# A two-block, one-core kernel: the second block's first norm scaled behind its matrix units, and a layer norm about a half mean

## What is computed

```
x1 = rmsnorm(x0, final_norm_g)                       # end of the first block
h  = rmsnorm(x1, l0_norm_mix)                        # start of the second
p  = h @ l0_w_in                                     # 14 x 128 columns of rwkv, then q, k, v of 512 each
p_rwkv = p_rwkv + (shift(p_rwkv) - p_rwkv) * mu      # shift: by one token
...
u  = glu(h4 @ pw1 + pw1_b)                           # second layer, 1024 channels
u  = causal depthwise conv of 31 taps over u, + dw_b
mean, var over the 1024 channels
u  = silu((u - mean) * rsqrt(var + 1e-5) * ln_w + ln_b)
x  = x + u @ pw2 + pw2_b
```

## Time and profile before

| | before |
|---|---|
| median of 3 | 995.29 us |
| profiled execution's own time | 994.44 us |
| its span | 992.6 us |
| mean granted clock of TensorE | 0.978 |
| PE busy | 936.7 us (94%) |
| DVE busy | 598.6 us (60%) |
| ACT busy | 456.6 us (46%) |
| POOL busy | 73.9 us (7%) |
| chain that ended last | PE 86%, DVE 5%, issue 3%, ACT 3% |

### The profile page before, as it was taken

How to read it: one execution, slowest core, us unless ns; L and a number is a source line. 1 busy time by engine, 2 the same in 40 slices (tenths; PEclk the granted TensorE clock), 3 DMA queues, 4 the chain that set the end, 5 groups by cost and what they waited for, 6 DMA issues and landing times.

```text
span 992.6 us, 16055 instructions
## 1 busy us (share of the span) xinstructions
PE 936.7 (94%) x6750; PEld 820.4 (83%) x6750; DVE 598.6 (60%) x771; ACT 456.6 (46%) x653; POOL 73.9 (7%) x150
## 2 busy tenths in 40 slices
PE   6999999999799998999899999997999699999995
PEld 5898799999699988878688888887975588888884
DVE  5456667556657866735476666565631866666663
ACT  6446555434467444421354444444422555444441
POOL 6000000000210030000000000000642000000000
PEclk9999999999999999989999999997999899999998
DMA  9754353556645531000156555654882146566521
GB/s 323 231 180 166 127 169 129 170 172 210 224 150 170 171 127 44 1 1 11 35 171 233 190 173 205 204 182 127 222 226 63 67 166 212 173 209 204 177 85 43
DMA packets 105943, 152.46 MB, mean 154 GB/s; under 512 B 4098, under 2 KB 82448, under 8 KB 105872
## 3 DMA queue, kind: packets, MB, share of 16 engines
q1 hardware_dynamic: 101424, 141.45, 43.8%
q0 software_dynamic: 4272, 9.85, 3.6%
q10 hardware_dynamic: 176, 0.14, 0.0%
HBM read 145.58 MB, written 1.06 MB: 148 GB/s over the span
## 4 chain that ended last, share of the span: by engine, by line
PE 86%; DVE 5%; issue 3%; ACT 3%; DMA 1%; POOL 1%; DVEq 0%; POOLq 0%; SPq 0%; ACTq 0%
PE banks L1715 17%; PE banks L1717 17%; PE banks L1716 17%; PE banks L1759 12%; PE banks L1760 6%; PE banks L2088 4%; PE banks L2287 3%; DVE wl L1045 1%; ACT wh L630 1%; PE banks L2176 1%; PE banks L1865 1%; PE banks L1840 1%; PE banks L1818 1%; DMA arena<-in_l_rel_bias 1%; PE banks L2187 1%
## 5 line engine op out<-in xcount | busy, mean ns | idle before, releaser
L1045 DVE TENSOR_TENSOR wl<-raw,wh 128x2048 fp32r<-128x2048 f32 x132 | 302.2, 2292 | 157.0 <-ACT wh L630 156.1
L630 ACT ACTIVATE wh<-raw 128x2048 fp32r<-128x2048 f32 x132 | 252.1, 1912 | 96.3 <-PE banks L1717 91.4
L1715 PE MATMUL banks<-x,wh 128*128 128x256 f32 x704 | 201.5, 286 | 2.5 <-DVE x L1099 2.3
L1716 PE MATMUL banks<-x,wh 128*128 128x256 f32 x704 | 198.8, 282 | 0.0
L1717 PE MATMUL banks<-x,wl 128*128 128x256 f32 x704 | 198.7, 282 | 0.0
L1759 PE MATMUL banks<-x,wh 128*128 128x512 f32 x512 | 179.3, 392 | 0.0
L1760 PE MATMUL banks<-x,wl 128*128 128x256 f32 x512 | 143.2, 280 | 0.0
L1715 PEld LDWEIGHTS banks<-x,wh 128*128 128x128 f32 x704 | 134.0, 190 | 7.8 <-issue 7.7
L1716 PEld LDWEIGHTS banks<-x,wh 128*128 128x128 f32 x704 | 134.1, 191 | 0.3 <-issue 0.2
L1717 PEld LDWEIGHTS banks<-x,wl 128*128 128x128 f32 x704 | 134.0, 190 | 0.0
L1715 PE MATMUL banks<-wh,yh 128*128 128x512 f32 x288 | 114.8, 399 | 3.0 <-DVE yl L1542 3.0
(11 more groups left out here) (320 smaller groups left out, 1198.7 us busy)
## 6 DMA issues: line engine op xcount, KB each, us to landing
raw<-in_l_ffn_up SPq DMA_DIRECT2D x32, 1024.0 KB, 5.5
raw<-in_l_ffn_down SPq DMA_DIRECT2D x32, 1024.0 KB, 5.0
raw<-in_w_in SPq DMA_DIRECT2D x29, 1024.0 KB, 5.2
raw<-in_l_w_in SPq DMA_DIRECT2D x13, 1024.0 KB, 5.1
raw<-in_l_pw SPq DMA_DIRECT2D x12, 1024.0 KB, 5.8
arena<-arena POOLq DMA_DIRECT2D x64, 71.0 KB, 3.7
raw<-in_w_out SPq DMA_DIRECT2D x4, 1024.0 KB, 5.1
raw<-in_l_w_out SPq DMA_DIRECT2D x4, 1024.0 KB, 5.0
```

The costliest lines, as they stand in the source:

```text
L630: nc.scalar.activation(wh[:, u % WBUFS, :], raw[:, u % RAWS, :], ACT.Copy).then_inc(E("hi_split"), 1)
L1045: nc.vector.tensor_tensor(wl[:, u % WBUFS, :], raw[:, u % RAWS, :], wh[:, u % WBUFS, :].bitcast(F32), ALU.subtract).then_inc(E("lo_split"), 1)
L1715: mm(out, hh, mh, start=start, stop=False)
L1716: mm(out, hh, ml, start=False, stop=False)
```

## The change

Two places are rewritten.

**The norm between the blocks.** `proj_out("wo")` gets `norm="n2"`: PE transposes the left half of `gained` (unscaled) between the halves of wo1, the right half behind it. Nothing scales the rows. DVE makes `row_diag`, the identity times `R12`; PE multiplies it by ones (`rb`, bank 4) after rw6, which gives `R12` along the free axis in all partitions, and DVE copies it to `row_tile`. Each rw unit, q2 and k2 is taken out of its bank by DVE times `row_tile`; v2 is scaled per partition by ACT. The mixing reads the scaled copy. rw6 runs in halves of the contraction. The lora loads move ahead of the band load on POOL.

**The layer norm.** The sum of the first four chunks times 2/1024, the mean of one half of the channels, is `ln_shift`. All chunks are shifted by it first, then sums and squares are taken while taps 2 and 3 run, on chunks added up by DVE; the variance is the mean square less the squared mean of the shifted values. Only then is the rest of the mean taken off, pair by pair, pair 1 on POOL. Taps 2 and 3 run in halves. The first two chunks go through affine, silu and split singly; the affines of the others are ACT's. `pw`'s first column half runs chunk by chunk for both row tiles. `pw2_b` is loaded before taps 1's shifts and added during taps 3.

The diff, cut to its core:

```diff
# POOL
+            pool.dma_start(lora[0:64, 0, :], A["l0_w2_2"]).then_inc(E("lora_loaded"), 16)   # and two more
             pool.wait_ge(E("gained"), 4)
             ...                                    # band load, wait, memset
-            wait_full(pool, "n2_t2")               # and n2_t3, then the three lora loads
+            pool.wait_ge(E("ln_deviation"), 1)
+            pool.wait_ge(E("ln_centred"), 2)
+            nc.gpsimd.tensor_tensor(acc[:, 2:4, :], acc[:, 2:4, :], rest2, ALU.subtract).then_inc(E("ln_pool_centred"), 1)
# ACT
-            for _ in range(3):
+            for _ in range(2):
                 next_unit()
+            split_norm("n2", (0, 1))
+            next_unit()
             squares("wo", gain=True)
-            split_norm("n2")
+            split_norm("n2", (2, 3))
             for n, u in enumerate(RW_ORDER):
                 next_unit()
-                wait_full(act, name)
+                wait_empty(act, f"rw{u}")
                 for j in range(2):
-                    nc.scalar.activation(thb[...], bank(name)[...], ACT.Copy, scale=mu)
+                    nc.scalar.activation(thb[...], scaled_rows[n % 2][...], ACT.Copy, scale=mu)
-                copy_out(q2[:, 2 * i:2 * i + 2, :], f"q2_{i}")       # k2 alike
+            copy_out(v2[:, 0, :], "v2_0", scale=R12[:, 0:1])
...
+            taps_out(1)
+            nc.scalar.activation(ln_shift, bank("lnc")[:, 0:T], ACT.Copy, scale=2.0 / DM)
+            mark(nc.scalar.activation(NMAX[:, 0:1], EPSL, ACT.Sqrt))
+            # squares of pairs 0, 1, 2, then of chunks 6 and 7
+            nc.scalar.activation(ln_mean_sq, bank("lnm")[:, 0:T], ACT.Square, scale=1.0 / DM)
+            nc.scalar.activation(ln_rest, bank("lnm")[:, 0:T], ACT.Copy, scale=1.0 / DM)
+            nc.scalar.activation(lnsd, lnsd, ACT.Sqrt, bias=EPSL).then_inc(E("ln_deviation"), 1)
+            ln_tanh(0), ln_tanh(1), ln_tanh(2)
+            ln_hi(0, 0, 1), ln_hi(1, 1, 1)
+            ln_tanh(3), ln_affine(2), ln_affine(3)
+            ln_hi(2, 2, 2)                          # then the same for pairs 2 and 3
# DVE
+                        if gain and c and s:
+                            next_unit_half(0)       # wl of a unit in two halves of 1024 columns
-            add_residual("wo", units=((1,), (2, 3)), gain=True)
+            add_residual("wo", units=((1,), (2,)), gain=True, norm="n2")
+            next_unit_half(1)
+            split_norm("n2", (2, 3))                # behind the small sums, ahead of row_diag
-                nc.vector.tensor_scalar(scratch[...], gained[...], R12[:, s:s + 1], None, ALU.mult)
-            split_norm("n2")
+                nc.vector.tensor_scalar(row_diag[:, s * P:(s + 1) * P], ident, R12[:, s:s + 1], None, ALU.mult)
+            nc.vector.tensor_copy(row_tile, bank("rb")[:, 0:T]).then_inc(empty("rb"), 1)
+            def scaled_out(dst, name):
+                wait_full(dve, name)
+                nc.vector.tensor_tensor(dst, chunks(bank(name)), rows2, ALU.mult).then_inc(empty(name), 1)
             for n, u in enumerate(RW_ORDER):
+                scaled_out(chunks(scaled_rows[n % 2]), f"rw{u}")
                 next_unit()
                 dve.wait_ge(E("mu_part"), 2 * n + 2)
                 ...                                 # the mix, from scaled_rows, counted in rows_mixed
             next_unit()
+            scaled_out(q2[:, 0:2, :], "q2_0")       # q2_1, k2_0, k2_1 alike, each behind a next_unit
...
-                build_taps(i)
+                if i < 3: build_taps(i)
+            # early sums of pairs 0 and 1 in two steps -> ln_early_sum; build_taps(3)
+            # shift pairs 0 and 1 by ln_shift; ln_late = ln_shift - dw_b, 4 chunks; pw2b added to xn, 2 rows
+            late_out("taps2", 4, 2)                 # 0.5 * bank - ln_late
+            # sum of chunks 4 and 5 -> ln_late_sum; squares of pairs 0, 1, 2 added up -> ln_square_sum
+            late_out("taps3", 6, 1)
+            late_out("taps3b", 7, 1)
+            nc.vector.scalar_tensor_tensor(out=lnsd, in0=bank("lnv")[:, 0:T], scalar=1.0 / DM, in1=ln_mean_sq,
+                                           op0=ALU.mult, op1=ALU.subtract)
+            centre(0)
+            mark(nc.vector.reciprocal(lnsd, lnsd))
+            ln_divide(0)
+            ln_divide(1)                            # waits for ln_pool_centred
+            steps = [ln_affine(c) for c in range(2)]
+            for c in range(2): ...; ln_silu(c, 1, ln_late)
+            ln_lo(0, 0, 1), ln_lo(1, 1, 1)
+            centre(2), ln_divide(2)
+            ln_pair(1)                              # silu of a pair
+            ln_lo(2, 2, 2)
+            centre(3), ln_divide(3)
+            ln_pair(2), ln_lo(3, 4, 2), ln_pair(3), ln_lo(4, 6, 2)
# PE
+                if source == "ln":
+                    order = [(s, k) for k in range(4) for s in range(NT)]
-            proj_out("wo", xh, xl, "merged")
-            norm_transposes("n2")
+            proj_out("wo", xh, xl, "merged", norm="n2")
-                t_unit(f"rw{u}", None if n else "n2")
+                t_unit(f"rw{u}", None if n else "n2", halves=not n)
+                if n == 0:
+                    pe.wait_ge(E("row_diag"), NT)
+                    give(mm(take("rb")[:, 0:T], const("ones"), row_diag, start=True, stop=True), "rb")
...
             conv_taps(1)
+            conv_half(2, 0, "taps2", True, False)
+            # wait ln_early_sum; lnc = ones x ln_sums
+            conv_half(2, 1, "taps2", False, True)
+            conv_half(3, 0, "taps3", True, True)
+            # wait ln_late_sum; lnm += ones x late sum; wait ln_square_sum; lnv += ones x ln_sq_sums
+            conv_half(3, 1, "taps3b", True, True)
+            # lnm += chunk 6; lnv += square 6; lnm += chunk 7; lnv += square 7
```

More of the change, by code:

```diff
@@ new lines, in _ @@
+            for k in range(2):
+                act.wait_ge(E("ln_centred"), k + 1)
+                ln_square(2 * k, 2)
+            wait_empty(act, "taps2")
+            ln_square(4, 2)
+            wait_empty(act, "taps3")
+            ln_square(6, 1)
+            wait_empty(act, "taps3b")
+            ln_square(7, 1)
+            wait_full(act, "lnm")
+            nc.scalar.activation(ln_mean_sq, bank("lnm")[:, 0:T], ACT.Square, scale=1.0 / DM).then_inc(E("ln_mean_sq"), 1)
+            nc.scalar.activation(ln_rest, bank("lnm")[:, 0:T], ACT.Copy, scale=1.0 / DM).then_inc(empty("lnm"), 1)
@@ L1386, in _ @@
             next_unit()
+            scaled_out(k2[:, 0:2, :], "k2_0")
             sync()
@@ L1662, in _ @@
+            for k in range(2):
+                nc.vector.tensor_tensor(pair(k), pair(k), on_pairs(ln_shift), ALU.subtract).then_inc(E("ln_centred"), 1)
+            for c in range(4):
+                ins = nc.vector.tensor_scalar(ln_late[:, c, :], ln_shift, vcol("l1_dw_b_2", 4 + c), None, ALU.subtract)
+                mark(ins)
             dve.wait_ge(E("pw2b_loaded"), 16)
@@ L1665, in _, with late_out @@
             sync()
+            def late_out(use, first, n):
+                wait_full(dve, use)
+                nc.vector.scalar_tensor_tensor(out=acc[:, first:first + n, :], in0=chunks(bank(use)[:, 0:n * T]), scalar=0.5,
+                                               in1=ln_late[:, first - 4:first - 4 + n, :], op0=ALU.mult, op1=ALU.subtract)\
+                    .then_inc(empty(use), 1)
+            late_out("taps2", 4, 2)
+            wait_empty(dve, "taps2")
+            nc.vector.tensor_tensor(ln_sums[:, T:2 * T], acc[:, 4, :], acc[:, 5, :], ALU.add).then_inc(E("ln_late_sum"), 1)
@@ L2282, in conv_taps, with conv_half @@
                 pe.wait_ge(E(f"rows_shifted{i % 3}"), 256 * (i // 3 + 1))
-                out = take(f"taps{i}")
                 for j in range(2):
-                    for g in range(TAP_GROUPS):
-                        for q in range(4):
-                            ins = mm(out[32 * q:32 * q + 32, j * T:(j + 1) * T], tap_blocks(i)[:, g, 4 * j + q, :],
-                                     shifted(i)[:, j, q, SHIFTS * g:SHIFTS * g + T], start=g == 0, stop=g == TAP_GROUPS - 1)
-                give(ins, f"taps{i}")
+                    conv_half(i, j, f"taps{i}", not j, j)
+            def conv_half(i, j, use, first, last):
+                out = take(use) if first else bank(use)
+                cols = slice(0, T) if first else slice(T, 2 * T)
+                for g in range(TAP_GROUPS):
+                    for q in range(4):
+                        ins = mm(out[32 * q:32 * q + 32, cols], tap_blocks(i)[:, g, 4 * j + q, :],
+                                 shifted(i)[:, j, q, SHIFTS * g:SHIFTS * g + T], start=g == 0, stop=g == TAP_GROUPS - 1)
+                if last:
+                    give(ins, use)
             for i in range(4):
```

279 lines of the change are left out of this document (170 added, 109 removed).

## The result

The changed kernel takes 980.26 us (median of 4 runs, 978.97 to 983.44), where the kernel before took 994.43 beside it (4 runs, 992.18 to 996.01): a ratio of 0.9862, interval 0.9841 to 0.9884, 14.2 us faster. Forecast were 985.3 us (10.0 faster) and a range down to 983.2, so the sign was right and the gain too small by 4.2 us. The profiled execution took 980.61 us, 978.8 of it span, at a mean granted clock of 0.984 (before: 994.44, 992.6, 0.978). One execution further down (1002.6 us, clock 0.965) fell into a slower state of the chip and is left out.

What follows compares the result with a forecast made beforehand. PE, busy 94% of the span, bounds the kernel, so time is won where it stands or runs slowly. Gains of 4.6 (norm) and 5.35 (layer norm) sum to 9.95: median 985.3 us from 995.29, range 983.2 to 989.8.

Steps and rivals of the forecast that it cites:

- first unit earlier: Norm between the blocks: unit rw6 starts at 270.65 in place of 276.96, 6.3 us earlier.
- stand ahead of `kn`, with what leads to it: Unit loop, n = 2: DVE's scaling and queued weight split delay the mix, so PE stands 1.1 us.
- `q2_0` leaves its bank late: Unit loop: q2_0 leaves its bank about 0.1 us after k2_0 wants it; bounds 0 and 1.0.
- part one: Norm between the blocks and unit loop: 4.6 us earlier in all, bounds 2.5 and 5.7.
- PE waits for the square sums: Layer norm, during the last taps: PE waits 0.9 us for DVE's sum of squares.
- the projection starts earlier: Layer norm: PE starts the projection at 771.6 in place of 778.26, 6.65 us earlier.
- given back in the chunks behind: Projection: later chunks and pw1's weights come late, with PE stands of 0.35 and 0.65 us.
- part two: Layer norm and its projection: 5.35 us earlier in all, bounds 3.0 and 6.3.
- The clock didn't fall ahead of the first unit (12%): Rival, 12%: clock falls in the 2.3 us between "wo" and rw6, costing 2.0 us: 987.3.
- DVE's queue (14%): Rival, 14%: in the unit loop narrow distances break or squares come late; part one gives 2.5 us: 987.4.
- Of the layer norm (12%): Rival, 12%: PE starts early but waits for later pairs and pw1's weights; 3.0 us in place of 5.35: 987.7.
- "Better than summed" (10%): Rival, 10%: no kn stand and no stands in the projection, 12.0 us gained: 983.3.
- The Trainium skill's rule on transposes: Ahead of rw6: transposes don't count as PE work "the same way" for the clock, which could fall from 268.35 to 270.65.
- the Trainium skill's rule on DVE and GpSimd: Layer norm: POOL's centring would wait for DVE's until 766.35, end at 767.55, still ahead of 768.75; cost nothing.

Runs made afterwards that it cites:

- again: The kernel before, run again unchanged: 994.14 us, ratio 0.9998.
- part two alone: The kernel before with only the layer norm's hunks of the change, the norm between the blocks as before: 988.45 us, ratio 0.9938.
- the parts alone: The kernel before with only the norm's hunks, 987.79 us (0.9934), and with only the layer norm's hunks, 988.45 us (0.9938).
- layer norm busy: The changed kernel with 13 unread ones-products between the layer norm's variance product and the projection: 979.48 us, ratio 0.9873.
- without the stands: The changed kernel with a weight split moved behind the mix and the projection's bias additions behind the last taps: 980.41 us, ratio 0.9860.
- late by 2.2 and 4.3: The changed kernel with 5 or 10 unread products behind the second block's first unit: 985.21 us (0.9897) and 986.2 us (0.9911).
- before kept busy: The kernel before with 17 unread products in five TensorE stands outside the changed stages: 988.94 us, ratio 0.9959.
- part two kept busy: The kernel before with only the layer norm's hunks, plus 17 unread products in five stands outside the changed stages: 983.86 us, ratio 0.9891.
- products at n4: The kernel before with only the 9 unread products around the fourth norm's transposes: 991.16 us, ratio 0.9972.
- before late: The kernel before with 10 unread products behind the second block's first unit: 997.18 us, ratio 1.0035.
- the last three runs: Unread products behind the second block's first unit: changed kernel with 5, 985.21 us, with 10, 986.2 us; kernel before with 10, 997.18 us.

## Why the prediction was right or wrong

| step of the prediction | forecast | by the two traces |
|---|---|---|
| first unit earlier | 6.3 | 6.4 (6.83 less the start's 0.42) |
| `rb`, in the open | 0.5 | 0.4 |
| stand ahead of `kn`, with what leads to it | 1.1 | 1.0, of it 0.91 as one wait |
| `q2_0` leaves its bank late | 0.1 | 0.4 |
| **part one** | 4.6 | 4.6 |
| PE waits for the square sums | 0.9 | 0.5 |
| the projection starts earlier | 6.65 | 6.8 (14.89 less 8.10) |
| given back in the chunks behind | 1.3 | 1.1 |
| POOL's centring | 1.2 | 1.26 |
| **part two** | 5.35 | 5.7 |
| all other stages | 0 | 3.5 |

The working of both parts held, nearly row by row. What made it hold is that every duration came from a row of the same shape, and that the queue behind each moved instruction was followed to who waits for it: the `kn` stand was found that way, by a few additions. Undoing its cause confirmed it. Some of the closeness is luck. The `kn` sum is added up wrongly: 0.1 + 0.68 + 2.29 + 0.88 is 3.95 and not 3.8, so the stand would be 1.25. And the last step of part two, 5.6 from 785.75, ends at 791.35 and not 791.5, which makes part two 5.5. Put right, the parts are 4.45 and 5.5, and their sum is 9.95 as before. (The lower bound of part one comes to 2.6 by its own terms, not 2.5.)

The step that failed is the one that is not written out. Under "Sum" the profiled execution's 994.44 us went into the forecast whole, so that the half clock outside the two parts, 29.6 of its 43 us (9.2 of them at the very end, where they cost neither kernel more than the other), counted as fixed. All other stages stood at 0, and measured 3.5 us; the bounds of the range had no term for them. In the runs that half clock is not fixed. The same kernel's stretches come and go from one execution to the next: with the same instructions up to 740 us, the clock over 424 to 444 was 0.83, 0.83 and 1.00 in the traces of the kernel before, of it again and of part two alone. The size of that: taking away from each run's ratio what its trace shows as added or removed, the change wins 13.7 and 15.2 (whole change), 12.8 (6.6 and 6.2, the parts alone), 12.4 (layer norm busy), 12.4 (without the stands), 12.4 and 13.2 (late by 2.2 and 4.3), each give or take 2.1 to 2.6 us. All lie above the 10.3 of path, by 2 to 5 us. Part of that is the first trace of the kernel before, which was a mild one in the touched stages too. Over the seven traces that have it, the old layer norm took 0.4 us longer than in the first (0 to 1.6); the new one is 5.9 shorter and not 5.7 on average of eight, the new norm 4.7 and not 4.6, and the old norm adds another 0.4 (below). So the path is worth about 11.4 on average.

Shown: 2.8 of the 3.5 us of the first two traces are TensorE's clock in stages that the change doesn't touch (-1.5, 3.0 and 1.3, each step of the staircase beside a stretch of half clock), and with the clock held there by products the gap is 11.0. The other 0.8, half of it before 256 and half from 698 to 740, have no such stretch beside them and stay unexplained. Shown in part: one source of it is the removed stand itself. In the seven traces of kernels with the old norm (before, again, part two alone, before kept busy, part two kept busy, products at n4, before late), its stretch of half clock lasted 3.4 to 10.2 us; twice it was 10.2, and then it reached into the first unit and cost 1.5 us more (with products at n4, PE is 0.22 ahead of the trace before at 276.96 and 1.25 behind at 335.6). That is 0.4 us on average, and the new norm has no such stretch. Open: whether the later stretches are shorter behind the new norm for a reason or by chance. At 678 the four traces of the old norm without products have 10.2 us each, the seven of the new norm 3.4 (three), 6.8 (one) and 10.2 (three). From 336 to 740 us the four come -1.8 to 1.8 us ahead of the first trace (mean 0.4), the seven -2.2 to 5.0 (mean 2.3); a difference of 1.8 with such spreads isn't clear of chance. Being earlier isn't enough (the kernel without stands had both in full), and the last three runs don't tell a shift from chance.

The rivals. The clock didn't fall ahead of the first unit (12%): PE's stand there was 1.36 us and not 2.3, with two transposes done in it. DVE's queue (14%) cost 0.4 in place of 0.1. Of the layer norm (12%) 1.1 us was given back and not 3.6. "Better than summed" (10%) is where the time ended, but by another way than it says: its stands were all there. The Trainium skill's rule on transposes that the prediction weighed (TensorE: Matmul & The Clock Gate, Part 4: PE-mode transpose) made no difference, as the clock was never low there. The prediction's reading that the trace disagrees with it holds for five of the seven traces of the old norm, where the clock was back before the first product; in the other two it came back at 280.6, some 4 us into the unit. Nor did the Trainium skill's rule on DVE and GpSimd (SBUF — State Buffer, Who interferes with whom): POOL's centring began at 758.36, after DVE's had ended at 758.28, and took 1.26. Whether POOL waited for that or for ACT's root, which ended at 758.22, the trace doesn't tell; it was done at 759.62, ahead of DVE's second division at 760.7.

## What to carry to other kernels

A sum over the path is only half of a forecast when the trace holds tens of us at half clock: list those stretches, price each by the back-to-back work of PE inside it (here a stretch of 10.2 us was worth 2.8, not 5.1), and put into the range that they come and go. One trace of the kernel before doesn't show how far. Where PE stands one to three us ahead of dense work and nothing can fill the stand, a few products that nobody reads are cheap: 17 of them were worth 4.0 us in the kernel before. When a wait is removed, name what stood hidden behind it; here the wait for `q2_0` grew from 0.4 to 0.6 us when the 0.9 ahead of `kn` was gone.

## What the runs showed of the hardware

- The granted clock is not a property of the kernel alone. Over 74 runs of the kernel before, the mean of a run lay between 0.975 and 0.985, and the time went with it, 989.7 to 998.7 us.
- Products of ones in stands of 1 to 3 us held the clock at 1.00 over windows in which it had averaged 0.83 to 0.91: at 472 to 490 in five traces of five with them and in none of eleven without, at 664 to 694 in six of six and in none of eleven.
- Between variance and projection ScalarE loads a table ahead of the tanh. It lies beside the reciprocal (758.25 to 760.0) and is hidden, by the timeline of the changed kernel:

```profile
757.71 0.51 ACT L1024 ACTIVATE arena<-arena,small 128x256 f32<-128x256 f32 x1 [0.29 <-DVE arena L1741]
758.24 1.28 ACT L1028 ACT_TABLE_LOAD   x1
```
